# TensorE transposes ahead of the newest scores, and DVE copies ahead of the row maximum, in the three-buffer attention stages

## The reference

```python
# first block, 8 heads of width 96, and 8 heads of width 64 with a table of log counts added
s = jnp.einsum('bqhd,bkhd->bhqk', q_blk, k).astype(jnp.float32) * scale
p = jax.nn.softmax(s, axis=-1).astype(v.dtype)
return jnp.einsum('bhqk,bkhd->bqhd', p, v)
...
# second block, neighbourhood heads: near keys with a bias, then the context keys
s_nb = jnp.where(in_win[:, None, :], s_nb, -jnp.inf)
p = jax.nn.softmax(jnp.concatenate([s_nb, s_cx], axis=-1), axis=-1)
```

## Time and profile before

| | |
|---|---|
| median of 3 runs | 4875.2 us (4872.27 to 4878.87) |
| the profiled execution | 4865.81 us, its span 4864.1 us |
| TensorE busy, share of the span | 3732.1 us, 77% |
| DVE, ScalarE busy | 2448.6 us (50%), 2216.1 us (46%) |
| steps of am, ad, ac (both layers) | 64, 64, 108 |
| am: TensorE idle before scores until DVE's copy (L1124) | 19.9 us, 57 times |
| ad: TensorE idle before the turned transpose until ScalarE's oT | 12.8 us, 32 times |
| mean granted TensorE clock | 0.889 of full speed |

### The profile page before, as it was taken

One profiled execution on the slowest core, in us unless ns is written; L12 is line 12 of the kernel. 1 busy time (PEld: TensorE's weight loads), 2 busy tenths in 40 slices (PEclk: granted clock), 3 DMA queues, 4 the chain that ended last, 5 costly groups with the idle time before them and its releaser, 6 DMA issues. The chain is left out here.

```text
span 4864.1 us, 71195 instructions
## 1 busy us (share of the span) xinstructions
PE 3732.1 (77%) x24823; PEld 3032.3 (62%) x24823; DVE 2448.6 (50%) x4501; ACT 2216.1 (46%) x3911; POOL 912.1 (19%) x749
## 2 busy tenths in 40 slices
PE   4497589788529999468997868765868997869657
PEld 3495377566428888357775657654657775658446
DVE  0303355343278788584443545555584444546564
ACT  0313455572127777432224656555332225657452
POOL 0021200000015665224460000000024450000002
PEclk7698799899659999779998999987989998989888
DMA  9334820421369999422222414152222223232333
GB/s 372 114 100 144 225 60 17 108 75 44 113 173 394 395 395 397 148 89 91 93 95 64 110 39 105 37 130 70 92 76 86 96 92 85 75 81 58 78 107 93
DMA packets 328051, 633.97 MB, mean 130 GB/s; under 512 B 115025, under 2 KB 171249, under 8 KB 326673
## 3 DMA queue, kind: packets, MB, share of 16 engines
q1 hardware_dynamic: 292220, 510.37, 33.4%
q0 software_dynamic: 33840, 113.66, 7.3%
q10 hardware_dynamic: 1636, 5.39, 0.3%
HBM read 490.39 MB, written 138.95 MB: 129 GB/s over the span
## 5 line engine op out<-in xcount | busy, mean ns | idle before, releaser
L1809 PE MATMUL pr_ps<-pr_wH,hT_part 128*128 128x512 f32 x1120 | 447.5, 400 | 0.0
L1579 ACT ACTIVATE ex_high<-ex_ring 128x2048 fp32r<-128x2048 f32 x192 | 368.6, 1920 | 95.6 <-PE ex_pg L1555 37.6
L1625 DVE TENSOR_TENSOR ex_ring_part<-ex_ring,ex_high 128x2048 fp32r<-128x2048 f32 x144 | 370.9, 2576 | 50.9 <-ACTq L1580 39.3
L1809 PE MATMUL pr_ps<-pr_wH,x_sb_part 128*128 128x512 f32 x896 | 366.7, 409 | 22.7 <-DVEq L1882 22.7
L1809 PE MATMUL pr_ps<-pr_w_part,x_sb_part 128*128 128x512 f32 x896 | 359.1, 401 | 0.0
L1116 DVE TENSOR_REDUCE aa_nm<-aa_ps 128x1 f32<-128x1280 f32 (+1 forms) x144 | 197.7, 1373 | 307.5 <-PE aa_ps L1030 306.7
L1520 POOL TENSOR_TENSOR ex_ring_part<-ex_ring,ex_high 128x2048 fp32r<-128x2048 f32 x48 | 238.6, 4971 | 215.0 <-ACTq L1580 215.0
L1040 PE MATMUL aa_ps<-ident,aa_prob 128*128 128x128 f32 x1312 | 209.7, 293 | 61.2 <-ACTq L1159 60.1
L1155 ACT ACTIVATE aa_prob<-aa_ps,aa_nm 128x512 f32<-128x512 f32 (+2 forms) x272 | 211.1, 776 | 88.4 <-DVEq L1117 44.5
L1809 PEld LDWEIGHTS pr_ps<-pr_wH,hT_part 128*128 128x128 f32 x1120 | 217.5, 194 | 47.9
L1116 DVE TENSOR_REDUCE ab_nm<-ab_ps 128x1 f32<-128x1280 f32 (+1 forms) x108 | 148.3, 1373 | 193.6 <-PE ab_ps L1030 193.2
(11 more groups left out here) (352 smaller groups left out, 9187.2 us busy)
## 6 DMA issues: line engine op xcount, KB each, us to landing
ex_ring<-in_w_gate SPq DMA_DIRECT2D x64, 1024.0 KB, 9.7
ex_ring<-in_w_up SPq DMA_DIRECT2D x64, 1024.0 KB, 8.3
ex_ring<-in_w_down SPq DMA_DIRECT2D x64, 1024.0 KB, 8.1
mod_w<-in_w_ada SPq DMA_DIRECT2D x24, 2048.0 KB, 12.8
z_d<-pr_zT POOLq DMA_DIRECT2D x120, 256.0 KB, 3.0
pr_w<-in_w_in SPq DMA_DIRECT2D x14, 2048.0 KB, 8.7
proj<-pr_raw POOLq DMA_DIRECT2D x60, 256.0 KB, 2.3
w_out<-in_w_out SPq DMA_DIRECT2D x3, 4096.0 KB, 18.8
```

The source lines that it names most:

```text
L1579: scalar.activation(wH[:, c % HL].bitcast(F32R), w_sb[:, c % SL], ACT.Copy)
L1625: vector.tensor_tensor(w_part[:, c % SL].bitcast(F32R), w_sb[:, c % SL], wH[:, c % HL], ALU.subtract)
L1809: mm = tensor.matmul(ps[:, g % 4, :], x.bitcast(F32R), w[:, c % 2, kk, :].bitcast(F32R), start=kk == 0 and i == 0, stop=kk == KC - 1 and i ...
```

## The change

In the stages with three buffers (`LAG == 2`), TensorE issues `transposes(g)` ahead of `scores(h)`, and DVE does the eviction of step g, now the function `turned_part`, ahead of the division and the maximum. In the stages with two buffers (`LAG == 1`) both orders stay. In all stages TensorE no longer signals `tr`, and DVE no longer waits for it, in a step of which DVE has no columns; `parts_before` counts the steps that have some. The numbers of instructions on data are the same, ScalarE's, SP's and POOL's lists are untouched.

```diff
--- before.py
+++ after.py
@@ -921,6 +921,9 @@
             c0, c1 = by_act(t)[1], spans[t][-1][1]
             return (max(c0, spans[t][-1][0]), c1) if c0 < c1 else None
 
+        def parts_before(g):
+            return sum(by_dve(t) is not None for _, t, _ in steps[:g])
+
         def starts(t):
             return (0, 512) if apart else itertools.accumulate([0] + [b - a_ for a_, b in tiles[t][:-1]])
 
@@ -1042,8 +1045,6 @@
                                 mm.then_inc(tr0, 1)
                         if by_dve(t):
                             mm.then_inc(tr, 1)
-                        else:
-                            credit(pe, tr, 1)
 
                     def values(m, second):
                         p, t, _ = steps[2 * m]
@@ -1068,10 +1069,12 @@
 
                     for h in range(n + 4 + LAG):
                         g = h - LAG
-                        if h < n:
+                        if h < n and LAG == 1:
                             scores(h)
                         if 0 <= g < n:
                             transposes(g)
+                        if h < n and LAG == 2:
+                            scores(h)
                         if g % 2 == 0 and g >= 4:
                             turned((g - 4) // 2)
                         if g % 2 == 0 and 2 <= g < n + 2:
@@ -1088,8 +1091,21 @@
                     prepare(dve)
 
                 def body(it):
+                    def turned_part(g):
+                        if 0 <= g < n:
+                            p, t, j = steps[g]
+                            if by_dve(t):
+                                dve.wait_ge(tr, it * parts_before(n) + parts_before(g + 1))
+                                cols = slice(*by_dve(t))
+                                vector.tensor_copy(pT[:, g // 2 % 2, j, cols], ps[g % SB][:, cols])
+                                dve.drain()
+                            credit(dve, evd, 1)
+
+
                     for h in range(n + 4 + LAG):
                         g = h - LAG
+                        if LAG == 2:
+                            turned_part(g)
                         if g % 2 and g >= 5:
                             m = (g - 5) // 2
                             p, t, _ = steps[2 * m]
@@ -1115,14 +1131,8 @@
                             else:
                                 vector.tensor_reduce(most, ps[h % SB][:, 0:count[t]], AX.X, ALU.max, negate=True)
                             dve.drain().then_inc(mx, 1)
-                        if 0 <= g < n:
-                            p, t, j = steps[g]
-                            dve.wait_ge(tr, it * n + (g + 1))
-                            if by_dve(t):
-                                cols = slice(*by_dve(t))
-                                vector.tensor_copy(pT[:, g // 2 % 2, j, cols], ps[g % SB][:, cols])
-                                dve.drain()
-                            credit(dve, evd, 1)
+                        if LAG == 1:
+                            turned_part(g)
                 iterate(dve, body)
 
             @block.scalar
```

## The result

The changed kernel takes **4921.1 us** (median of 4 runs, 4916.4 to 4925.7) against 4876.6 us of the kernel before beside it (4 runs, 4872.3 to 4878.9): a ratio of 1.0094, with a 95% interval of 1.0078 to 1.0110. It is 44.5 us slower. Three executions of the experiments took two to three times as long as the others of their kernel (15083.4 us of before, 9606.8 and 11417.4 us of the kernel with DVE's part alone); no figure here uses them, and nothing on record shows what held them up. The profiled execution took 4919.3 us, span 4917.7; that of before took 53.6 us less in span.

A forecast was written before the change was run, and what follows sets the result against it. Chains of waits were taken to set am's pace (scores, maximum, copy, scores), ScalarE to bound ad, DVE to be tight in ac. Longer new chains add 3.9 + 9.4 + 20.5 + 1.8 = 35.6 us: 4911 us, range 4890 to 4938.

The forecast's parts named there:

- The old ring goes: Scores, DVE's maximum, copy, next scores: 7.72 us a pair of slots in am; the change cuts this chain of waits.
- a second one grows: Chain oT, turned, values, transposes, scores, maximum, exp, oT closes once a pair; transposes newly in it; 6.47 us before in am.
- am: Stage whose pair of slots was to go from 7.72 to 7.87 us, +0.15 on 26 pairs: +3.9 us.
- ad: Stage without a DVE copy; pair to go from 6.87 to 7.23 us, +0.36 on 26 pairs: +9.4 us.
- ac: Stage in both layers; full-tile pair from 6.21 to 6.78 us: +20.5 us, plus 1.8 for first and last tiles.
- The third rival: TensorE's clock falls in ac, another sixth of the time at the lower level: +16 us, 4927; chance 0.10.
- 18 us of allowance: Margin to either side for misread starts, 0.2 us a pair on 88 pairs: 4893 to 4929.
- The drain: Estimated 0.42 us hold after DVE's copy would make am's term 12 us; held contradicted by the rows, not used.
- The open second ring: Rival: oT is done when TensorE reaches the turned transpose, only engines' own work is left: 4802 us; chance 0.10.
- The balance of rings: Rival: each ring overstated by 0.4 us a pair, so no change: 4875 us; chance 0.08.

The follow-up runs named there:

- DVE's part alone: The change with TensorE back in its old order (scores ahead of transposes), DVE's new order kept: 5039.8 us in its profiled execution, 5049.7 in one other.
- the first experiment: The change plus ScalarE taking oT in the odd slot, ahead of its exp, in three-buffer stages: 4781.1 us, ratio 0.9814 to the kernel before.
- The filled wait: The change plus six matmuls of 512 columns, result unread, in ac before TensorE's wait for oT: 4901.8 us, ratio 1.0052 to the kernel before.

## Why the prediction was right, and where it was off

4921 us lies in the range of 4890 to 4938 and 10 above the forecast; slower by over 0.2% had 0.81.

**The old ring goes, a second one grows.** Right, and shown from both sides: by the rows of after, and by the first experiment, which opens the second ring and gets 90 us in place of the cost of 44.5.

**am.** The term was 3.9, the stage has +7.3. Seven of the ring's eight pieces came within 0.03 us; the division, taken at 1.10 between its bounds of 0.97 and 1.24, took 1.22 (703.78 to 705.00). The row nearest to it, ac's 1.24, should have been taken as it stood, its idle time included. The 26 steady pairs add up to 7.2 us more than before: most are at 7.98, and one in each iteration at 8.32. So nearly all of the term is in them, and filling and draining cancel to 0.1 us.

**ad.** The term was 9.4, the stage has +5.0. The pair is 7.10 and not 7.23, and nearly all of that is one piece: transposes to the next matmul, 0.96 in before, is 0.85 when scores follow (1043.69 to 1044.54). The 0.96 had been read where the values followed. The 26 steady pairs give +5.7, the ends of the iterations −0.7.

**ac.** The term was 22.3, the stages have +36.9. The ring was right, 6.85 for 6.78. What was mis-sized is the clock: the sum gave it nothing. The third rival had it at 16 us on top, with a chance of 0.10. Its size came from another sixth of the time at the lower level, a fall of the granted clock by 0.08 for which it had no rows; the clock fell by 0.06 to 0.10. The filled wait shows 17.4 us. With it, ac is 346.4 us at 0.97 and 0.96, 18.7 over before, which is the ring's part, less the little that before itself lost at 0.92 and 0.94. The reason given against the rival was that ac's waits are about a microsecond; that held for before. The ring that the prediction itself had summed leaves TensorE idle in one piece in front of the turned transpose, and the length of that piece was never worked out. It could have been: in before TensorE is busy for 4.27 us of a pair (4689.4 to 4695.6 us), and the ring's 6.78 less that is 2.5, the wait of 2.56 that came.

**Sum.** 35.6 forecast; 49.2 in the traces, 44.5 between medians. Forecast less measured, am's error is −3.4 and ad's +4.4, and they cancel; ac's ring was put 3.6 too high; the clock's 17.4 is the rest. That 4911 stands only 10 under the result is in part luck: the 18 us of allowance were meant for misread starts, and it was the missing clock that they had to hold.

**The drain.** By the Trainium skill, "VectorE: DVE Perf Modes", section "The DRAIN you can't avoid", am's term would have been 12 us, in the prediction's reading of it. In after the copy runs 0.69 us and the division starts 0.12 after it (702.97, 703.78), so an estimate with 0.42 is wrong here, as the rows of before had said. But the prediction quoted the rule without its exception: the same section says that a next operation that is not held starts earlier. The rows fit that sentence and don't contradict the page.

**The rivals.** The open second ring (4802) didn't come, but its paces, 7.13, 6.41 and 5.1, were met within 0.2 us when the ring was opened. The balance of rings (4875) fell with the paces of after. The clock came in part beside the forecast, not in place of it.

## What to carry to other kernels

When a reorder cuts the ring that sets the pace, write down the next ring before building it, sum it piece by piece from rows with the same neighbours, and look for the cheapest piece that can be taken out of it: here two edits, one worth 0.4% and the other less than nothing alone, gave 1.9% together. Then work out how long each engine stands in one piece in the new ring. A wait that grows in TensorE can cost its clock as well, and a clock that fell can be told from a longer ring by filling the wait with matmuls whose result nobody reads.

## What was not expected of the hardware

Matmuls that are of no use make a kernel faster: some 160 records more in ac of layer 0 (1163 for 1002) and 125 in layer 1, inside a wait, raised the granted clock from 0.86 and 0.84 to 0.97 and 0.96 and gave 16.3 us. And am, which has 0.97 before and after with typical waits under 0.8 us a pair, fell to 0.90 in the kernel with DVE's part alone, where TensorE waits 2.14 us before the turned transpose (709.47 us). There the level changes from pair to pair: many pairs run wholly at full clock (1.00 from 624.5 to 633.4 us) and the next at 0.84.
